# A bias added by one-partition matmuls into PSUM instead of by VectorE, in the spatial gate of a fused two-block kernel

## The chip, the cores and the metric

The kernel runs on one core of a Trainium2 chip. The metric is the device time of one execution in microseconds (us), as the median of several runs.

## The reference

The reference runs two network blocks on a sequence of 1024 tokens with 1024 channels. The first block has attention, a bidirectional mLSTM and a mixture of experts. The second block has an even layer and an odd layer. The change touches one part of the even layer, the spatial gate. With `u`, `v` and `g_b` as column groups of `rmsnorm(x) @ w_in`, of 1024 columns each:

```
vg = v.reshape(Bn, nc, CHUNK, B_GROUPS, B_GROUP_DIM)      # 8 chunks of 128 tokens, 4 groups of 256 channels
w = where(tril, ws, 0)                                     # (4, 128, 128)
mixed = einsum('gts,bnsgc->bntgc', w, vg) + bs.T[None, None, :, :, None]
y_b = u * mixed * silu(g_b)
x = x + concat([y_a, y_b]) @ w_out
```

The bias `bs[g, t]` depends on the group and on the token's place in its chunk, and is the same for all channels of the group.

## The kernel before, in words

`phase_even` is written with one hand-ordered instruction queue for each engine, tied by semaphores. Activations are channel-major: 128 channels in the partitions, 1024 tokens in the free dimension.

**The projection.** The input projection is cut into `PAIRS = 20` pairs of 128-channel tiles. Each pair `m` is computed as seven "products" of half-size blocks (a Strassen-like scheme, class `Quarters`). GpSimd (POOL) and ScalarE (ACT) split the weights into a high and a low part; TensorE (PE) runs 12 matmuls of 128x512 for each product (L2619 to L2621); ACT takes out the first product (`p1`) and VectorE (DVE) the others (`u2`, `u3`, `c21`, `c22_u4`, `c11`, `c12`, all L2635). Four PSUM banks take the products in turn, so a late eviction on DVE can hold up PE.

**The order of pairs.** Pairs 0 to 7 belong to the pooling part. Then there are four "triples" `j` (one for each spatial group), pairs `8+3j` (`v_cm`), `9+3j` (`g_cm`) and `10+3j` (`u_cm`). Small work is put between the products of these pairs:

- behind products 0 and 1 of the second pair, PE transposes `v` chunk by chunk (`turn_v`, L3017) into the PSUM tiles `aux` and `acc`, and DVE copies them to `v_rows_` (L3298);
- behind products 1 to 4 of the third pair, PE calls `mix_spatial(j, t, b)` (L3026), 16 calls in all. Each call runs four f32 matmuls of 128x128 with 128 moving columns, one for each of four chunks, into one bank;
- in the first pair of the next triple, DVE runs `gate_spatial` (L3304, `u * silu(g)`) and `mixed_out` for `t = 0, 1`: one add of the bias (L3312), which reads PSUM and writes `g_cm`, and one multiplication (L3315), into `gated`. For the last triple this stands behind all products, and `lo_of_y` (L3319) follows it, which makes the low parts that the out-projection (L3065) reads.

**The bias.** At the start of the phase one matmul with a ones row as weights (L2992) spreads the bias over all 128 partitions in `aux[:, 0]`. DVE copies it to `bias_rows` (L3335) between `u3(0)` and `c21(0)`, next to the copy of the transposed mixing weights (L3336).

**The out-projection.** It runs 16 units of 48 matmuls. The third unit (k = 2) is the first to need rows 8 to 15 of y, the last two of which come from the last triple.

Of the kernel before, what the change touches and what calls it, by code (L numbers as in the profile page):

```python
# [16 lines left out]
ALU = mybir.AluOpType  # L17
# [3 lines left out]
P = 128  # L21
LINE = 128
D = 1024
KT = D // P
# [9 lines left out]
CHUNK = 128  # L34
XCH = SEQ // CHUNK
# [14 lines left out]
CONST_AT, _n = {}, 0  # L50
# [106 lines left out]
class PhaseSemaphores:  # L157
# [25 lines left out]
    def sem(self, name):  # L183
        self.used.append(self.nc.alloc_semaphore(name, num=self.sets[0][len(self.used)]))
        return self.used[-1]

def build_program(nc, A, out):
    with ExitStack() as ctx:
        phases = PhaseSemaphores(nc)  # L190
        sem = phases.sem
# [10 lines left out]
        start = (nc.sbuf_base + LINE - 1) // LINE * LINE  # L202
# [20 lines left out]
        def cst(name):  # L223
            at, width = CONST_AT[name]
            return const[:, at:at + width]
# [9 lines left out]
        ident, ones = cst("ident"), cst("ones")  # L235
# [2446 lines left out]
        def phase_even(first_z):  # L2682
# [4 lines left out]
            G, POOL_PAIRS, TRIPLES = len(POOL_SIZES), 2 * len(POOL_SIZES), KT // 2  # L2687
# [39 lines left out]
            ws_t = mem("spat_ws_t", [P, G, CHUNK])  # L2727
# [3 lines left out]
            ws_low = ws_mem("spat_ws_low", [P, G, CHUNK])  # L2731

            v_cm = Arena(nc, a_at[0])("spat_v_cm", [P, 2, SEQ])
            v_rows_ = Arena(nc, a_at[1])("spat_v_rows", [P, 2, XCH, P])
            g_cm = Arena(nc, sums_at)("spat_g_cm", [P, 2, SEQ])
            u_cm = Arena(nc, pooled_at)("spat_u_cm", [P, 2, SEQ])
            gated = Arena(nc, y_at)("spat_gated", [P, 2, SEQ])
            bias = Arena(nc, start + 4 * CONST_AT["near_mask"][0])("spat_bias", [1, G, CHUNK])
            bias_rows = Arena(nc, start + 4 * CONST_AT["near_mask"][0])("spat_bias_rows", [P, G, CHUNK])
            assert G * CHUNK <= CONST_AT["near_mask"][1] + CONST_AT["chunk_mask"][1]  # L2740

            KO, EARLY = 2 * KT, 3
# [48 lines left out]
            masked = sem("spat_masked")  # L2792
            ws_turned = sem("spat_ws_turned")
            ws_ready = sem("spat_ws_ready")
            bias_out = sem("spat_bias_out")
            biased = sem("spat_biased")
            v_turned = sem("spat_v_turned")
            rows_out = sem("spat_rows_out")
            spat_silu = sem("spat_silu_done")
# [3 lines left out]
            y_done = sem("even_y_done")  # L2803
# [37 lines left out]
            def unit(k):  # L2841

                if k < 4:
                    return k % 2, KT * (k // 2)
                return k // 2, KT * (k % 2)

            with nc.psum_tensor("even_z", [P, 2, HALF], F32) as second_z, nc.psum_tensor("even_aux", [P, 2, HALF], F32) as aux, \
# [94 lines left out]
                def _(pe):  # L2942
# [45 lines left out]
                    spread_out(3)  # L2988
                    pe.wait_ge(masked, 1)
                    for g in range(G):  # L2990
                        pe.transpose(aux[:, 1, g * CHUNK:(g + 1) * CHUNK], ws_low[:, g, :], ident)
                    pe.matmul(aux[:, 0, :], ones[0:1, :], bias[:].rearrange("p g t -> p (g t)"), start=True, stop=True).then_inc(ws_turned, 1)  # L2992

                    def multiply(m, i, between=None):
                        if m == 0:
# [24 lines left out]
                    def mix_spatial(j, t, b):  # L3020
                        to = (aux, acc)[t]
                        pe.wait_ge(rows_out, 2 * j + t + 1)
                        if j == 0:
                            pe.wait_ge(ws_ready, 1)
                        for c in range(4):
                            ins = pe.matmul(to[:, b, c * CHUNK:(c + 1) * CHUNK], v_rows_[:, t, 4 * b + c, :], ws_t[:, j, :], start=(c == 0), stop=(c == 3))  # L3026
                        if b == 1:
                            ins.then_inc(spat_mixed, 1)

# [21 lines left out]
                    for k in range(2 * KT):  # L3051
                        n, first = unit(k)
# [6 lines left out]
                        for kt in range(KT):  # L3059
                            c = first + kt  # L3060
                            if k in (0, 2):
                                pe.wait_ge(y_lo_done, c + 1)
                            for w, rhs, begin, end in ((wo_hi, y_hi[c], c == 0, False), (wo_hi, y_lo[c], False, False), (wo_lo, y_hi[c], False, c == KO - 1)):
                                for b in range(2):
                                    ins = pe.matmul(z[n % 2][:, b, :], w[:, u, kt], rhs[:, b * HALF:(b + 1) * HALF], start=begin, stop=end)  # L3065
# [3 lines left out]
                def _(act):  # L3069
# [44 lines left out]
                    for m in range(PAIRS):  # L3114
                        g, j, kind = m // 2, (m - POOL_PAIRS) // 3, (m - POOL_PAIRS) % 3
                        if m == 0:
                            act.wait_ge(pads_clear, 1)
                        if m < POOL_PAIRS and m % 2 == 0 and g >= 2:
                            act.wait_ge(pooled_done, 2 * (g - 1))
                        if m < POOL_PAIRS and m % 2:  # L3120
                            act.wait_ge(y_done, 2 * g)
                        if m >= POOL_PAIRS:
                            if j == 0:
                                act.wait_ge((pooled_done, pooled_done, y_done)[kind], (2 * (G - 1), 2 * G, KT)[kind])
                            elif kind == 0:
                                act.wait_ge(v_turned, 2 * j)
                            else:
                                act.wait_ge(gated_done, j)
                            if j and kind == 1:

                                act.wait_ge(y_done, KT + 2 * j)
                        quarters.p1(act, m, banks, targets(m))
                        hi(m, 0)
                        if m < POOL_PAIRS + 1 and m % 2 == 0 and m:
                            act.wait_ge(quarters.evicted, 7 * (m - 1) + 7)
                            act.activation(silu[:], silu[:], ACT.Silu).then_inc(pool_silu, 1)
                        if m >= POOL_PAIRS and kind == 2:
                            act.wait_ge(quarters.evicted, 7 * (m - 1) + 7)
                            act.activation(g_cm[:], g_cm[:], ACT.Silu).then_inc(spat_silu, 1)
                        hi(m, 1)  # L3140
                        hi(m, 2)
                        if m < POOL_PAIRS and m % 2 and g:
                            store_y(2 * (g - 1), y)
                        if m >= POOL_PAIRS and kind == 1:
                            if j == 0:
                                store_y(KT - 2, y)
                            else:
                                store_y(KT + 2 * (j - 1), gated)
                        hi(m, 3)
                        hi(m, 4)  # L3150
                        hi(m, 5)
                        hi(m, 6)
# [32 lines left out]
                def _(dve):  # L3185
# [120 lines left out]
                    def mixed_out(j, t):  # L3306
                        dve.wait_ge(spat_mixed, 2 * j + t + 1)
                        dve.wait_ge(gated_done, j + 1)
                        if j == 0:
                            dve.wait_ge(bias_out, 1)  # L3310
                        mixed = g_cm[:, t, :]
                        dve.tensor_tensor(mixed.rearrange("p (c t) -> p c t", t=CHUNK), (aux, acc)[t][:].rearrange("p b (c t) -> p (b c) t", t=CHUNK),  # L3312
                                          bias_rows[:, j, :].unsqueeze(1).to_broadcast([P, XCH, CHUNK]), ALU.add).then_inc(biased, 1)
                        dve.wait_ge(biased, 2 * j + t + 1)
                        dve.tensor_tensor(gated[:, t, :], mixed, gated[:, t, :], ALU.mult).then_inc(y_done, 1)  # L3315

                    def lo_of_y(c):
                        dve.wait_ge(y_hi_done, c + 1)
# [2 lines left out]
                    for g in range(G):  # L3321
                        m = 2 * g
                        u2(m)
                        if g == 0:
                            token_lo(B21, b21)
                        u3(m)
                        if g == 0:
                            token_lo(B22, b22)

                            dve.wait_ge(t_lo_done, 7)  # L3330
                            step(dve.memset(sums[:, :, 0:PAD], 0.0))
                            step(dve.memset(a_pad[1][:, :, 0:PAD], 0.0))
                            dve.wait_ge(ws_turned, 1)
                            dve.wait_ge(x_stored, 16 * GROUPS)
                            dve.tensor_copy(bias_rows[:], aux[:, 0, :].rearrange("p (g t) -> p g t", g=G)).then_inc(bias_out, 1)  # L3335
                            dve.tensor_copy(ws_t[:], aux[:, 1, :].rearrange("p (g t) -> p g t", g=G)).then_inc(ws_ready, 1)  # L3336
                        c21(m)
                        c22_u4(m)
                        c11(m)
                        if g:  # L3340
                            gate_pool(g - 1)
                        c12(m)
                        m = 2 * g + 1
                        pool_part(g, 0)
                        u2(m)
                        pool_part(g, 1)
                        u3(m)
                        pool_part(g, 2)
                        c21(m)
                        pool_part(g, 3)  # L3350
                        c22_u4(m)
                        pool_part(g, 4)
                        c11(m)
                        pool_part(g, 5)
                        c12(m)
# [1087 lines left out]
```

## Time and profile before

| | |
|---|---|
| median of 3 runs | 3379.95 us (3379.56 to 3381.2) |
| profiled execution | 3379.95 us, span 3377.9 us |
| PE busy | 3125.4 us, 93% of the span |
| DVE busy | 1851.4 us, 55% |
| ACT, POOL busy | 38%, 48% |
| mean granted TensorE clock | 0.962 of full speed |
| even layer's first product to its last out-projection matmul | 1256.46 to about 1877 us of the span |

The span runs from the first to the last instruction of the profiled execution. Busy shares are averages over stages with different limits, so the stretch of the change has to be read by itself. PE matmuls are pipelined: a record of 0.39 us can start 0.23 us after the one before, so costs are read from distances between starts, not from durations. Records that follow one another are merged, with their count (x8). A f32 matmul shows as two records (two passes), and a f32r one or a transpose as one.

### The profile page before, as it was taken

The page shows a single profiled execution, that of the slowest core. Times are in us where ns is not written, and L with a number is a line of the kernel's source. Part 1 is how long each engine was busy: PE and PEld are TensorE (multiplying, and loading weights), DVE is VectorE, ACT ScalarE, POOL GpSimd, SP SyncE. Part 2 cuts the span into 40 slices and gives each one's busy share as a digit, 9 for nine tenths or more (in the row PEclk, how much of TensorE's full clock was granted, in tenths as well). Part 3 has the DMA queues.
Part 4 walks back from the last instruction along what each step waited for, and adds up shares of the span by engine and source line. Part 5 has one row for each costly group of instructions (what it writes and reads, how often), then busy time and mean ns, then how long its engine had stood idle before and what let it go on. Part 6 is the DMA issues. An engine that isn't in the chain of part 4 may idle for free. (4 is left out here: it accounts for less than half of the span.)

```text
span 3377.9 us, 43503 instructions
## 1 busy us (share of the span) xinstructions
PE 3125.4 (93%) x15972; PEld 2573.3 (76%) x15972; DVE 1851.4 (55%) x2678; ACT 1269.4 (38%) x2146; POOL 1611.9 (48%) x1056
## 2 busy tenths in 40 slices
PE   4979997969599969999999799999999999999999
PEld 3767786757388837778888588888888888888887
DVE  5566223662699856544361665555556556555712
ACT  5256122741477732222220343443344444222311
POOL 2331231123312217777743465565566556688732
PEclk8989998979799979999999899999999999999999
DMA  8230112035599961222251111111111111222331
GB/s 291 47 88 21 49 43 78 28 105 195 187 378 396 395 193 54 74 67 81 72 187 64 50 48 47 54 51 44 48 48 51 50 41 54 82 63 81 110 106 69
DMA packets 312571, 353.89 MB, mean 105 GB/s; under 512 B 28488, under 2 KB 280300, under 8 KB 306101
## 3 DMA queue, kind: packets, MB, share of 16 engines
q1 hardware_dynamic: 301182, 311.36, 27.5%
q0 software_dynamic: 4608, 16.78, 2.0%
q10 hardware_dynamic: 6582, 23.13, 1.7%
q8 instruction: 123, 2.02, 0.2%
q14 instruction: 76, 0.61, 0.1%
HBM read 293.28 MB, written 54.53 MB: 103 GB/s over the span
## 5 line engine op out<-in xcount | busy, mean ns | idle before, releaser
L2584 POOL TENSOR_TENSOR odd_quarter_lo<-odd_w_sums,odd_quarter_hi 128x512 fp32r<-128x512 f32 x224 | 300.3, 1342 | 278.2 <-ACT odd_quarter_hi L2579 276.7
L2619 PE MATMUL first_z<-odd_t_hi,odd_quarter_hi 128*128 128x512 f32 x784 | 327.5, 418 | 18.1 <-DVE odd_t_lo L4073 18.1
L2619 PE MATMUL odd_z<-odd_t_hi,odd_quarter_hi 128*128 128x512 f32 x784 | 325.5, 415 | 1.1 <-POOL odd_quarter_lo L2584 1.1
L2584 POOL TENSOR_TENSOR odd_quarter_lo<-odd_raw,odd_quarter_hi 128x512 fp32r<-128x512 f32 x168 | 232.0, 1381 | 167.4 <-ACT odd_quarter_hi L2579 163.0
L2621 PE MATMUL first_z<-odd_t_hi,odd_quarter_lo 128*128 128x512 f32 x784 | 308.3, 393 | 0.0
L2620 PE MATMUL first_z<-odd_t_lo,odd_quarter_hi 128*128 128x512 f32 x784 | 307.1, 392 | 0.0
L2621 PE MATMUL odd_z<-odd_t_hi,odd_quarter_lo 128*128 128x512 f32 x784 | 307.0, 392 | 0.0
L2620 PE MATMUL odd_z<-odd_t_lo,odd_quarter_hi 128*128 128x512 f32 x784 | 305.5, 390 | 0.0
L2579 ACT CAST odd_quarter_hi<-odd_w_sums 128x512 fp32r<-128x512 f32 x224 | 139.7, 624 | 365.6 <-PE odd_z L2621 178.8
L2635 DVE SCALAR_TENSOR_TENSOR dil_set<-first_z,dil_set 128x512 f32<-128x512 f32 x196 | 170.6, 884 | 143.3 <-PE first_z L2621 138.8
L2635 DVE SCALAR_TENSOR_TENSOR dil_set<-odd_z,dil_set 128x512 f32<-128x512 f32 x196 | 170.7, 884 | 138.4 <-PE odd_z L2621 133.5
L2579 ACT CAST odd_quarter_hi<-odd_raw 128x512 fp32r<-128x512 f32 x168 | 104.5, 622 | 293.9 <-PE first_z L2621 149.3
L275 POOL TENSOR_TENSOR w_hi<-w_raw,zero_col 128x1024 fp32r<-128x1024 f32 x25 | 47.4, 1895 | 303.1 <-PE mls_z L310 205.4
L2619 PEld LDWEIGHTS first_z<-odd_t_hi,odd_quarter_hi 128*128 128x128 f32 x784 | 148.5, 189 | 45.1 <-DVE odd_t_lo L4073 18.9
L2621 PEld LDWEIGHTS first_z<-odd_t_hi,odd_quarter_lo 128*128 128x128 f32 x784 | 148.2, 189 | 32.9
L2621 PEld LDWEIGHTS odd_z<-odd_t_hi,odd_quarter_lo 128*128 128x128 f32 x784 | 147.0, 187 | 32.5
L2620 PEld LDWEIGHTS first_z<-odd_t_lo,odd_quarter_hi 128*128 128x128 f32 x784 | 148.8, 190 | 26.9
L2619 PEld LDWEIGHTS odd_z<-odd_t_hi,odd_quarter_hi 128*128 128x128 f32 x784 | 147.6, 188 | 27.4 <-POOL odd_quarter_lo L2584 1.5
L2620 PEld LDWEIGHTS odd_z<-odd_t_lo,odd_quarter_hi 128*128 128x128 f32 x784 | 147.8, 189 | 26.5
L2584 POOL TENSOR_TENSOR even_quarter_lo<-even_w_sums,even_quarter_hi 128x512 fp32r<-128x512 f32 x80 | 110.5, 1385 | 72.0 <-ACT even_quarter_hi L2579 70.8
L2335 POOL DMA_INDIRECT ffn_rows<-expert_y,slot_token x16 | 32.6, 2040 | 219.6 <-ACT expert_y L2437 219.6
L4151 DVE COPY dil_p_t<-odd_aux 128x128 f32<-128x128 f32 (+1 forms) x192 | 67.6, 352 | 121.0 <-PE odd_aux L3736 100.2
(602 smaller groups left out, 8213.8 us busy)
## 6 DMA issues: line engine op xcount, KB each, us to landing
odd_raw<-in_odd_w_in SPq DMA_DIRECT2D x224, 256.0 KB, 3.1
raw_gate<-in_w_gate SPq DMA_DIRECT2D x16, 2048.0 KB, 15.0
raw_up<-in_w_up SPq DMA_DIRECT2D x16, 2048.0 KB, 14.8
raw_down<-in_w_down SPq DMA_DIRECT2D x16, 2048.0 KB, 15.2
even_raw<-in_even_w_in SPq DMA_DIRECT2D x80, 256.0 KB, 3.3
start_w_mod<-in_w_mod SPq DMA_DIRECT2D x11, 1024.0 KB, 10.8
w_raw<-in_w_in SPq DMA_DIRECT2D x16, 512.0 KB, 5.2
scan_w_mod<-in_w_mod SPq DMA_DIRECT2D x8, 1024.0 KB, 11.2
```

The source lines that it names most:

```text
L275: pool.tensor_tensor(w_hi[:, u], w_raw[:, u], zero_col[:, 0:1].to_broadcast([P, KT * P]).rearrange("p (k n) -> p k n", k=KT), ALU.add).the ...
L2335: pool.indirect_dma_start(ffn_rows, bass.IndirectOffsetOnAxis(ap=slot_token[:, e:e + 1], axis=0), y[:, e % 2, :], None, bounds_check=SEQ - ...
L2579: act.copy(self.w_hi[:, n % self.SLOTS], self.source(m, i)).then_inc(self.hi_done, 1)
L2584: pool.tensor_tensor(self.w_lo[:, n % self.SLOTS], self.source(m, i), self.w_hi[:, n % self.SLOTS].bitcast(F32), ALU.subtract).then_inc(se ...
L2619: pe.matmul(to, self.w_hi[:, slot, kt], t_hi[:, kt], start=(kt == 0), stop=False)
L2620: pe.matmul(to, self.w_hi[:, slot, kt], t_lo[:, kt], start=False, stop=False)
L2621: ins = pe.matmul(to, self.w_lo[:, slot, kt], t_hi[:, kt], start=False, stop=(kt == KT // 2 - 1))
L2635: dve.scalar_tensor_tensor(out=out, in0=product, scalar=scale, in1=more, op0=ALU.mult, op1=ALU.add).then_inc(self.evicted, 1)
L4151: dve.tensor_copy(p_t[:, u % 2, 0:w], turned[:, 0:w]).then_inc(free, 1)
```

## The change

The bias is no longer spread at the start of the phase and added by DVE. Each `mix_spatial` call first runs four matmuls that write the bias into the same PSUM places (weights: one row of 128 ones in one partition; moving data: the 128 bias values of group `j` in that partition), and then its four matmuls accumulate onto them. `mixed_out` keeps one instruction, a multiplication that reads PSUM. The matmul and the copy that spread the bias, the tile `bias_rows`, two semaphores and one wait of ACT are gone.

```diff
@@ PE, start of the phase
                     for g in range(G):
-                        pe.transpose(aux[:, 1, g * CHUNK:(g + 1) * CHUNK], ws_low[:, g, :], ident)
-                    pe.matmul(aux[:, 0, :], ones[0:1, :], bias[:].rearrange("p g t -> p (g t)"), start=True, stop=True).then_inc(ws_turned, 1)
+                        ins = pe.transpose(aux[:, 1, g * CHUNK:(g + 1) * CHUNK], ws_low[:, g, :], ident)
+                    ins.then_inc(ws_turned, 1)
@@ PE, mix_spatial
                         for c in range(4):
-                            ins = pe.matmul(to[:, b, c * CHUNK:(c + 1) * CHUNK], v_rows_[:, t, 4 * b + c, :], ws_t[:, j, :], start=(c == 0), stop=(c == 3))
+                            pe.matmul(to[:, b, c * CHUNK:(c + 1) * CHUNK], ones[0:1, :], bias[:, j, :], start=(c == 0), stop=False)
+                        for c in range(4):
+                            ins = pe.matmul(to[:, b, c * CHUNK:(c + 1) * CHUNK], v_rows_[:, t, 4 * b + c, :], ws_t[:, j, :], start=False, stop=(c == 3))
@@ ACT, main loop
-                            if j and kind == 1:
-
-                                act.wait_ge(y_done, KT + 2 * j)
@@ DVE, mixed_out
-                        if j == 0:
-                            dve.wait_ge(bias_out, 1)
-                        mixed = g_cm[:, t, :]
-                        dve.tensor_tensor(mixed.rearrange("p (c t) -> p c t", t=CHUNK), (aux, acc)[t][:].rearrange("p b (c t) -> p (b c) t", t=CHUNK),
-                                          bias_rows[:, j, :].unsqueeze(1).to_broadcast([P, XCH, CHUNK]), ALU.add).then_inc(biased, 1)
-                        dve.wait_ge(biased, 2 * j + t + 1)
-                        dve.tensor_tensor(gated[:, t, :], mixed, gated[:, t, :], ALU.mult).then_inc(y_done, 1)
+                        dve.tensor_tensor(gated[:, t, :], (aux, acc)[t][:].rearrange("p b n -> p (b n)"), gated[:, t, :], ALU.mult).then_inc(y_done, 1)
@@ DVE, start of the phase
                             dve.wait_ge(x_stored, 16 * GROUPS)
-                            dve.tensor_copy(bias_rows[:], aux[:, 0, :].rearrange("p (g t) -> p g t", g=G)).then_inc(bias_out, 1)
                             dve.tensor_copy(ws_t[:], aux[:, 1, :].rearrange("p (g t) -> p g t", g=G)).then_inc(ws_ready, 1)
```

## Rows read from the trace of the kernel before

**Rows 1.** The page: span, and PE's granted clock in 40 slices.

```profile
span 3377.9 us, 43503 instructions
...
PEclk8989998979799979999999899999999999999999
```

**Rows 2.** The triples: length, busy us (records) of PE, PEld, DVE, ACT, POOL; PEclk; DMA.

```profile
1470.00:1702.00 232.00, 232.00 (x1120) 194.79 (x1119) 93.42 (x106) 64.09 (x96) 166.92 (x118) 1.00 0.26 84
```

**Rows 3.** Waits of PE alone, 1300 to 1875: us in total, times, longest.

```profile
PE even_acc L3007 <- issue: 1.0, 1, 1.0
PE even_z L2619 <- POOL even_quarter_lo L2584: 0.4, 1, 0.4
```

**Rows 4.** Timeline around the first mix_spatial call: start us, us, engine, line.

```profile
1497.07 1.09 PEld L3026 LDWEIGHTS even_aux<-spat_ws_t,spat_v_rows 128*128 128x128 f32 x8
1497.30 1.06 PE L3026 MATMUL even_aux<-spat_ws_t,spat_v_rows 128*128 128x128 f32 x8
...
1498.11 0.48 PE L2619 MATMUL first_z<-even_t_hi,even_quarter_hi 128*128 128x512 f32 x1
...
1498.42 0.40 PE L2620 MATMUL first_z<-even_t_lo,even_quarter_hi 128*128 128x512 f32 x1
```

**Rows 5.** Timeline, DVE: evictions that wait for products of the third pair.

```profile
1508.44 1.29 DVE L2635 SCALAR_TENSOR_TENSOR spat_u_cm<-even_z,spat_u_cm 128x512 f32<-128x512 f32 x2 [2.95 <-PE even_z L2621]
...
1512.08 0.69 DVE L2635 SCALAR_TENSOR_TENSOR spat_u_cm<-even_z,spat_u_cm 128x512 f32<-128x512 f32 x1 [2.35 <-PE even_z L2621]
...
1514.80 0.69 DVE L2635 SCALAR_TENSOR_TENSOR spat_u_cm<-first_z,spat_u_cm 128x512 f32<-128x512 f32 x1 [2.03 <-PE first_z L2621]
```

**Rows 6.** Timeline, PE, start of the phase: matmuls on thin operands.

```profile
1228.72 3.61 PE L2956 MATMUL even_aux<-even_sq,const 128*1 128x256 f32 x16
...
1250.78 1.12 PE L2992 MATMUL even_aux<-spat_bias,const 1*128 1x512 f32 x2
1256.46 0.80 PE L2619 MATMUL first_z<-even_t_hi,even_quarter_hi 128*128 128x512 f32 x1 [4.56 <-DVE even_t_lo L3211]
```

**Rows 7.** Instructions by tile: count, ns min/median/max, first and last start.

```profile
L2992 PE MATMUL even_aux<-spat_bias,const x2: 587/640/692, 1250.8 to 1251.3; 1*128 1x512 f32 x2
...
L3315 DVE TENSOR_TENSOR spat_gated<-spat_g_cm,spat_gated x8: 1225/1724/1906, 1524.9 to 1715.1; 128x1024 f32<-128x1024 f32 x8
...
L3312 DVE TENSOR_TENSOR spat_g_cm<-even_aux,spat_bias_rows x4: 1217/1218/1225, 1523.6 to 1711.4; 128x1024 f32<-128x1024 f32 x4
```

**Rows 8.** Timeline, the first mixed_out, an eviction behind it, ACT's next p1.

```profile
1523.64 1.22 DVE L3312 TENSOR_TENSOR spat_g_cm<-even_aux,spat_bias_rows 128x1024 f32<-128x1024 f32 x1
...
1533.84 0.69 DVE L2635 SCALAR_TENSOR_TENSOR spat_v_cm<-even_z,spat_v_cm 128x512 f32<-128x512 f32 x1 [1.75 <-PE even_z L2621]
...
1536.64 0.60 ACT L2632 ACTIVATE spat_g_cm<-first_z 128x512 f32<-128x512 f32 x1 [2.18 <-PE first_z L2621]
```

**Rows 9.** Timeline, three engines, around the copy of the bias.

```profile
1284.53 0.69 DVE L3335 COPY spat_bias_rows<-even_aux 128x512 f32<-128x512 f32 x1
...
1286.90 1.28 POOL L2584 TENSOR_TENSOR even_quarter_lo<-even_raw,even_quarter_hi 128x512 fp32r<-128x512 f32 x1
...
1288.24 0.50 PE L2619 MATMUL even_z<-even_t_hi,even_quarter_hi 128*128 128x512 f32 x1 [0.75 <-POOL even_quarter_lo L2584]
```

**Rows 10.** Timeline behind the last product: third and fourth out-projection unit, last y_lo.

```profile
1711.40 1.23 DVE L3312 TENSOR_TENSOR spat_g_cm<-even_aux,spat_bias_rows 128x1024 f32<-128x1024 f32 x1
...
1725.67 6.25 DVE L3319 TENSOR_TENSOR even_y_lo<-spat_gated,even_y_hi 128x1024 fp32r<-128x1024 f32 x2
...
1724.30 0.61 PE L3065 MATMUL first_z<-even_y_hi,even_wo_hi 128*128 128x512 f32 x2
...
1735.22 0.62 PE L3065 MATMUL even_z<-even_y_hi,even_wo_hi 128*128 128x512 f32 x2
```

**Rows 11.** Stretches, PE alone: length, busy us (records), PEclk, DMA share, GB/s.

```profile
1250.00:1252.00 2.00, 1.90 (x8) 0.98 0.00 0
1256.00:1262.00 6.00, 5.49 (x12) 0.50 0.55 167
```

More of the change, by code:

```diff
@@ L2738, in phase_even @@
             bias = Arena(nc, start + 4 * CONST_AT["near_mask"][0])("spat_bias", [1, G, CHUNK])
-            bias_rows = Arena(nc, start + 4 * CONST_AT["near_mask"][0])("spat_bias_rows", [P, G, CHUNK])
-            assert G * CHUNK <= CONST_AT["near_mask"][1] + CONST_AT["chunk_mask"][1]
             KO, EARLY = 2 * KT, 3
@@ L2794, in phase_even @@
             ws_ready = sem("spat_ws_ready")
-            bias_out = sem("spat_bias_out")
-            biased = sem("spat_biased")
             v_turned = sem("spat_v_turned")
```

## The prediction

> **What bounds the kernel now.** I read the page first: its span, and the granted clock of TensorE by slices, which from the sixteenth slice on is at 9 (the full level of 2.4 GHz) in all slices but one [rows 1]. Then the stretch of the change in the even layer, to see which engine is full where the change acts. Between 1470 and 1702 us, the four triples, PE is busy for 232.00 of 232.00 us at a granted clock of 1.00, while DVE is busy for 93.42, ACT for 64.09 and POOL for 166.92 [rows 2]. Then the waits of PE by themselves from 1300 to 1875 us: two, 1.4 us together, neither behind a DVE instruction [rows 3]. So in the stretch of the change PE is the bound, and the other engines run behind it. Last I looked at single calls on the timeline, to price one pass of a small f32 matmul.
>
> The change gives PE work and takes work from DVE. All follows from that: what is added lies where nothing hides it, and what is removed lies under PE.
>
> **The cost on PE.** Four f32 matmuls are added to each of 16 `mix_spatial` calls: 64 matmuls. A call's four matmuls stand in the trace as eight records [rows 4], so 64 matmuls are 128 passes, each with a weight load of its own.
>
> What is a pass worth? I take it three ways.
> - By starts: the eight passes begin at 1497.30, and the second matmul of the next product at 1498.42 [rows 4]. That is 1.12 us, of which one ordinary product matmul is 0.227 (a product of 12 matmuls takes 1514.80 - 1512.08 = 2.72 us [rows 5]). It leaves 0.895 us for eight passes, 0.112 each.
> - By cadence: with a call between, a product's end comes 1512.08 - 1508.44 = 3.64 us after the last; without one, 2.72 [rows 5]. The call costs 0.92 us, 0.115 a pass. 
> - Low bound: the changeover lies within that cost. If all of the difference between the next product's first two starts (1498.11 and 1498.42 [rows 4], 0.31 us) and 0.227 is changeover, about 0.085 us, the eight passes are worth 0.81 us, 0.101 each.
>
> Those passes have 128 rows; the new ones have one. The nearest row is the matmul that is removed, which has the very same weights (one row of ones) and the same data in one piece. Its two passes of 512 columns take 1.12 us together [rows 6], with 0.587 to 0.692 for one record [rows 7]. So the distance between their starts is 0.43 to 0.53 us, and for 128 columns 0.107 to 0.133. Its granted clock was 0.98 [rows 11], so this is at the same level. A second thin shape, with one column of weights, takes 3.61 us for 16 passes of 256 columns [rows 6], with one record at 0.38 some 0.215 apart, or 0.107 for 128 columns. Neither thin shape is cheaper by columns than a full one; columns count, not rows. I take 0.112 us.
>
> 128 x 0.112 = 14.3 us. Bounds: 128 x 0.101 = 12.9, and 128 x 0.133 = 17.0 us.
>
> The Trainium skill gives the sustained distance for a stream of load and matmul pairs with 128 moving columns as about 81 ns (page "TensorE: Matmul & The Clock Gate", section "Back-to-back issue gap"); by that the sum would be an estimated 128 x 0.081 = 10.4 us. The figure is for one-pass data, and the trace of this kernel has 0.112 for a pass of f32; the row decides.
>
> **What is removed on PE.** The spreading matmul, 1.12 us at 1250.78 [rows 6], goes. PE then waits for `token_lo` on DVE until 1256.46 [rows 6], which the removal doesn't move: zero. If that wait were gone, it would be worth 1.1 us.
>
> **What is removed on DVE.** Eight adds of 1.22 us, 9.7 us; eight waits for them of 0.03 to 0.04, 0.3 us. The eight multiplications now take one operand from PSUM. I price them at the 1.22 us of the add, which also reads PSUM, instead of a median of 1.72 (two operands in SBUF) [rows 7]: some 4.0 us less. The copy of the bias is 0.6 us by starts [rows 9]. Together 14.6 us of DVE time, and on the path 0:
> - In the first three triples, the work of `mixed_out` starts at 1523.64, and DVE has caught up at 1533.84, where it waits 1.75 us for a product again [rows 8]. In between it was late, but PE did not wait for a bank [rows 3]. The cover is PE's own stream through four banks.
> - The last triple's adds lie behind all products, at 1711.40, and lead to the low parts of rows 14 and 15 of y, done at 1731.9. The third out-projection unit starts at 1724.30 and takes 10.92 us, or 1.365 for each row of y, so it needs the last row at 1724.30 + 7 x 1.365 = 1733.9 [rows 10]. That is 2.0 us of slack already. DVE waits there for PE's products, which come later by the added passes together with the unit, so the slack only grows. If it were gone, 2.9 us would be at stake.
> - The copy sits ahead of `c21(0)`. PE's next stop, at 1288.24, is released by POOL's split of 1286.90, not by an eviction [rows 9]. Zero; 0.6 us if it were an eviction.
>
> ACT loses a wait for `y_done`. The first one it stood ahead of begins at 1536.64, behind 2.18 us of waiting for PE's product [rows 8], so nothing is released. No DMA is added or moved; the loads of weights and of y go by PE's progress and shift with it. Behind the even layer everything hangs on the end of PE's last unit, and so the delay is carried to the end in full.
>
> **The sum.** The profiled execution took 3379.95 us, which is also the median of the runs shown; its span is 3377.9, with 2.05 us around it. 3379.95 + 14.3 - 0 = 3394.3 us. With the bounds: 3392.9 to 3397.0.
>
> **The rivals.**
> - *DVE gives it back.* If the evictions behind `mixed_out` did hold PE up through the banks, in each triple and at the end, the 14.6 us would come back: 3379.95 + 14.3 - 14.6 = 3379.7, no change. This decides only if PE has idle time of that size in the triples. It has none that the trace shows [rows 2, 3]. Matmul ends are modelled, so a hold of a few tenths could hide in a record, but the cadence of 2.72 us is that of undisturbed products [rows 5]. Chance 0.05, of which 0.02 on the faster side.
> - *Cheap passes.* If a pass over one partition ran at the rate of the product matmuls, 0.227 / 4 = 0.057 us for 128 columns [rows 5], the cost would be 7.3 us: 3387.2. For it: only one row of the array is fed. Against it: the removed matmul with the same operands [rows 6, 7]. Chance 0.05; it sits on the 0.2% line, so I halve it.
> - *Exposed weight loads.* If the loads did not run beside the matmuls of the other shape, each new pass would pay 0.187 us more (one load record of the call is 0.19, and eight spread over 1.09 us beside the matmuls [rows 4]): 128 x (0.112 + 0.187) = 38.3 us, 3418.2. In this kernel the loads do overlap where all rows are in use, since eight passes fit into less time than eight load durations. The Trainium skill says that weight loads overlap with matmuls in flight only when their row group differs (same page, "Part 3: Packing small matmuls", section "The mechanism"). A one-row matmul shares its row group with the full ones. The trace already contradicts the rule for full matmuls. Chance 0.03.
> - *The clock falls.* If the thin matmuls counted as rest and the granted clock went to its low level of 1.2 GHz behind each call, a product would take 5.49 instead of 2.72 us [rows 5, 11]: 16 x 2.8 + 14.3 = 59 us, 3439. At 1250 to 1252 us, with a thin matmul running, the clock was 0.98, and it was 0.50 only behind a gap of 4.6 us [rows 6, 11]. Chance 0.03.
>
> **How the numbers follow.** Forecast 0.84, rivals 0.16. A change within 0.2%, or 6.8 us, is about what a measurement of this kernel can't tell from none. Slower: 0.84 + 0.03 + 0.03 + 0.025 = 0.925. Same: 0.03 + 0.025 = 0.055. Faster: 0.02. The predicted time is the likeliest case, 3394.3. The range takes the bounds of the pass, 3392.9 and 3397.0, and about 2 us more on each side, a little over the spread of the runs shown (1.6 us): 3391 to 3399. It leaves out the rivals, 0.16.
>
> **What the profile after would show.** In the triples 128 new PE records of a one-row matmul, 8 ahead of each group of 8, and a distance between the product ends around a call of 3.64 + 0.90 = 4.54 us instead of 3.64. PE busy for all of the triples, its granted clock 1.00. The stretch from the first call to the end of the products is longer by 14.3 us; before and behind it, distances are as before. On DVE, L3312's adds are gone, the multiplications take 1.2 us, and its time without work is greater by about 14.3 + 14.6 = 28.9 us. Wrong would be: products that come closer together in the first pair of a triple than now (DVE did hold PE), passes 0.06 or 0.3 us apart, or a slice with a lower PEclk in the triples. A pass price other than 0.112 moves the sum by 1.28 us for each 0.01.

## The result, and the profile after

The changed kernel takes 3400.89 us (median of 4 runs, 3399.9 to 3401.98), the kernel before 3380.24 us (4 runs, 3379.56 to 3381.2) on the same chip. The ratio is 1.0061, with a 95% interval of 1.0046 to 1.0077. It is slower, as forecast, but by 20.7 us instead of 14.3, and 1.9 us above the range. The profiled execution took 3399.32 us.

The first two lines are the page's span and granted clock, and then come the stretch of the triples and the waits of PE in the even layer. They answer to [rows 1 to 3].

```profile
span 3397.2 us, 43746 instructions
...
PEclk8989998989799979999999899999999999999999
```

```profile
1470.00:1721.00 251.00, 251.00 (x1243) 207.93 (x1242) 82.10 (x99) 63.61 (x95) 162.12 (x119) 1.00 0.25 79
```

```profile
PE even_acc L3003 <- issue: 1.0, 1, 1.0
PE even_z L2619 <- POOL even_quarter_lo L2584: 0.4, 1, 0.4
```

PE is still busy for all of the triples, at a clock of 1.00, and has the same two waits as before. So there is no new wait and no lower clock: the added time is inside the stream of PE. From the first call to the first matmul of the out-projection it is 1721.14 - 1495.82 = 225.3 us; before, it was 205.2. That is 20.1 us more. The whole loss sits in the 16 calls. This stretch is a better measure than the span of one execution: the first call starts 1.5 us earlier here than before (1495.82 and 1497.30), and over all the traces of this document it starts anywhere from 1495.8 to 1502.4 us, whatever the calls cost.

How it is spread over them is seen on DVE, whose evictions wait for each product. These rows answer to [rows 5].

```profile
1500.84 0.69 DVE L2635 SCALAR_TENSOR_TENSOR spat_u_cm<-first_z,spat_u_cm 128x512 f32<-128x512 f32 x1 [4.22 <-PE first_z L2621]
...
1505.74 0.69 DVE L2635 SCALAR_TENSOR_TENSOR spat_u_cm<-first_z,spat_u_cm 128x512 f32<-128x512 f32 x1 [4.22 <-PE first_z L2621]
...
1515.56 0.69 DVE L2635 SCALAR_TENSOR_TENSOR spat_u_cm<-even_z,spat_u_cm 128x512 f32<-128x512 f32 x1 [3.62 <-PE even_z L2621]
...
1518.28 0.69 DVE L2635 SCALAR_TENSOR_TENSOR spat_u_cm<-first_z,spat_u_cm 128x512 f32<-128x512 f32 x1 [2.03 <-PE first_z L2621]
```

With a call between, products end 1505.74 - 1500.84 = 4.90 us apart (4.91 over the four calls of a triple), against 3.64 before and 4.54 forecast. Without a call it is 1518.28 - 1515.56 = 2.72 us, as before. A call costs 1.26 us more instead of 0.90, and 16 x 1.26 = 20.2 us.

Now one call from within: PE, and then PE's weight loads, around the first call. These answer to [rows 4].

```profile
1495.51 0.39 PE L2621 MATMUL even_z<-even_t_hi,even_quarter_lo 128*128 128x512 f32 x1
1495.82 1.15 PE L3022 MATMUL even_aux<-spat_bias,const 1*128 1x128 f32 x8
1496.91 1.16 PE L3024 MATMUL even_aux<-spat_ws_t,spat_v_rows 128*128 128x128 f32 x8
1497.82 0.48 PE L2619 MATMUL first_z<-even_t_hi,even_quarter_hi 128*128 128x512 f32 x1
...
1495.28 0.19 PEld L2621 LDWEIGHTS even_z<-even_t_hi,even_quarter_lo 128*128 128x128 f32 x1
1495.82 0.96 PEld L3022 LDWEIGHTS even_aux<-spat_bias,const 1*128 1x128 f32 x8 [0.35 <-issue]
1496.90 0.97 PEld L3024 LDWEIGHTS even_aux<-spat_ws_t,spat_v_rows 128*128 128x128 f32 x8
```

Three things are to be seen.

- Before, the first weight load of the call started 0.23 us ahead of its matmul, beside the matmuls of the product [rows 4]. Here the load of the bias starts at 1495.82 together with its matmul, with 0.35 us of idle time ahead, and the load of the first full matmul starts at 1496.90, 0.01 ahead. The loads don't run ahead where the weights go from 128 rows to one and back.
- The first bias matmul starts 0.31 us behind the last of the product, where 0.227 is the ordinary distance.
- The eight bias passes take 1496.91 - 1495.82 = 1.09 us instead of 0.895, and the eight full ones 1497.82 - 1496.91 = 0.91 instead of 0.81 [rows 4].

That is 0.08 + 0.195 + 0.10 = 0.38 us in all, about 0.19 for each of the two changes. The tile's rows say where a part of it sits (count, then ns at least, median and most):

```profile
L3022 PEld LDWEIGHTS even_aux<-spat_bias,const x64: 181/187/187, 1495.8 to 1704.6; 1*128 1x128 f32 x64
L3022 PE MATMUL even_aux<-spat_bias,const x64: 270/270/372, 1495.8 to 1704.7; 1*128 1x128 f32 x64
...
  issue: 5.6, 16
```

The first bias pass of a call takes 372 ns and the others 270; of the full passes behind them the first takes 377 and the others 275. The idle time of "issue" is 5.6 us in 16 pieces, one for each call.

On DVE the multiplication went as priced. These rows answer to [rows 8] and [rows 7]:

```profile
1527.13 1.21 DVE L3304 TENSOR_TENSOR spat_gated<-even_aux,spat_gated 128x1024 f32<-128x1024 f32 x1
1529.16 0.69 DVE L2635 SCALAR_TENSOR_TENSOR spat_v_cm<-first_z,spat_v_cm 128x512 f32<-128x512 f32 x1 [0.82 <-PE first_z L2621]
```

The multiplication takes 1.21 us (1.22 estimated), and DVE has caught up right behind it. At the tail, the last low parts of y and the start of the third out-projection unit, which answer to [rows 10]:

```profile
1741.42 2.35 DVE L3308 TENSOR_TENSOR even_y_lo<-spat_gated,even_y_hi 128x1024 fp32r<-128x1024 f32 x2
...
1742.90 0.62 PE L3063 MATMUL first_z<-even_y_hi,even_wo_hi 128*128 128x512 f32 x2
```

The low parts are done at 1743.8, and the last row of y is needed at 1742.90 + 7 x 1.365 = 1752.5. The slack grew from 2.0 to 8.7 us. A part of that was not priced: the two low parts take 2.35 us together, where they took 6.25 before [rows 10]. It is most of what DVE's busy time fell by beyond the forecast (1851.4 to 1832.7 us, 18.7 instead of 14.6). DVE is off the path, so it is worth nothing here, and no run asks for its cause.

### The profile page after: what moved, and what is told of

Its sections match the earlier page's. It is cut to its first block and busy times, and to the rows that moved or that the text cites. A ratio compares the mean times of both kernels' runs of the same rounds, so it can differ in the third digit from the quotient of the medians.

```text
span 3397.2 us, 43746 instructions
## 1 busy us (share of the span) xinstructions
PE 3144.3 (93%) x16098; PEld 2585.6 (76%) x16098; DVE 1832.7 (54%) x2669; ACT 1268.6 (37%) x2146; POOL 1598.9 (47%) x1056
```

## The experiments

All are edits of the changed kernel; the diffs show the lines that matter, and "..." stands for what is left out. Theory A, with its later forms, is that going over between weights of one row and of 128 costs time. The rivals were that accumulation onto a written bank costs, that a one-row pass is dear by itself, and that DVE's removed work was worth something. The measure of a call is the distance between product ends around it ("cadence": 3.64 before, 4.91 after).

**All 128 rows.** The same four bias matmuls with 128 rows of weights; rows 1 to 127 of the bias tile are zero.

```diff
+                    pool.memset(bias[:], 0.0).then_inc(bias_clear, 1)
...
-                            pe.matmul(to[:, b, c * CHUNK:(c + 1) * CHUNK], ones[0:1, :], bias[:, j, :], start=(c == 0), stop=False)
+                            pe.matmul(to[:, b, c * CHUNK:(c + 1) * CHUNK], ones[0:128, :], bias[0:128, j, :], start=(c == 0), stop=False)
```

> The changed kernel, but with the bias matmuls on all 128 rows: weights are the full tile of ones, and the moving tile holds the bias in row 0 and zeros in rows 1 to 127. Same count of passes and columns, same accumulation. Theory A (each change between one-row and 128-row weights costs about 0.19 us on PE, two for each of 16 calls, 6.1 us in all): the extra goes away, a call adds 0.90 us to the cadence, 16 x 0.90 = 14.3, so about 3394.7 us, 6 us below the changed kernel. Theory B (accumulating onto places just written costs the extra): no change from the changed kernel, 3400.9. Theory C (each one-row pass is itself slow, 1.26 / 8 = 0.158 us): also about 3394.7, so A and C are told apart by the next run.

3393.79 us (3391.38 to 3396.23, 5 runs) beside 3381.37 of before, 1.0037 (1.0023 to 1.0051). The cadence is 4.52. PE and the weight loads around its first call:

```profile
1497.45 0.39 PE L2621 MATMUL even_z<-even_t_hi,even_quarter_lo 128*128 128x512 f32 x1
1497.68 1.05 PE L3025 MATMUL even_aux<-spat_bias,const 128*128 128x128 f32 x8
1498.57 1.06 PE L3027 MATMUL even_aux<-spat_ws_t,spat_v_rows 128*128 128x128 f32 x8
1499.38 0.48 PE L2619 MATMUL first_z<-even_t_hi,even_quarter_hi 128*128 128x512 f32 x1
...
1497.46 1.08 PEld L3025 LDWEIGHTS even_aux<-spat_bias,const 128*128 128x128 f32 x8
```

The load runs 0.22 us ahead, the bias block takes 0.89 us and the full one 0.81. This is the forecast of the prediction (4.54), met with 128 times as many rows. Accumulation is ruled out as a cost, and so is the number of passes. What is left has to do with the one row.

**Two calls' bias together.** The call for bank 0 writes the bias of both banks, so that a pair of calls has two changes instead of four.

```diff
-                        for c in range(4):
-                            pe.matmul(to[:, b, c * CHUNK:(c + 1) * CHUNK], ones[0:1, :], bias[:, j, :], start=(c == 0), stop=False)
+                        if b == 0:
+                            for d in range(2):
+                                for c in range(4):
+                                    pe.matmul(to[:, d, c * CHUNK:(c + 1) * CHUNK], ones[0:1, :], bias[:, j, :], start=(c == 0), stop=False)
```

> The changed kernel, but the bias matmuls of both banks of a PSUM tile are issued together ahead of the first of the two calls: as many one-row passes as before, half as many blocks of them. Theory A (change of row count): 16 changes fewer, 16 x 0.19 = 3.0 us less, about 3397.8 us. Theory B (accumulation): the first call keeps it, the second has its places written earlier, so at most 8 x 0.19 = 1.5 us less. Theory C (slow one-row passes): no change, 3400.9.

3401.13 us (3399.63 to 3405.67, 5 runs), 1.006 (1.0047 to 1.0074): no gain, where theory A forecast 3397.8. Yet the cadences of the first triple are 5.81 and 3.64, or 9.45 for a pair against 9.81, which is the 0.36 of two changes saved. Eight pairs should have given 2.9 us. Where they went is seen in the stretches of PE in the second triple (length, busy us and records, clock, DMA share, GB/s):

```profile
1576.00:1578.00 2.00, 2.00 (x17) 1.00 0.00 0
1579.50:1582.00 2.50, 2.50 (x9) 0.50 0.80 225
1582.00:1584.00 2.00, 2.00 (x12) 0.99 0.37 112
```

Behind the 16 one-row passes the granted clock falls to 0.50, the level of 1.2 GHz, though PE never stopped, and it does so again in the third triple; behind the other six of the eight pairs it stays at 1.00. The stretch from the first call to the out-projection takes 225.6 us, where 225.3 - 2.9 = 222.4 was due, so the two falls cost 3.2 us. The saving is real and is given back by the clock.

**No bias at all.** The bias matmuls are left out, and with them the bias from the computation.

```diff
-                            pe.matmul(to[:, b, c * CHUNK:(c + 1) * CHUNK], ones[0:1, :], bias[:, j, :], start=(c == 0), stop=False)
```

> The changed kernel with the bias left out of the computation altogether: no bias matmuls, and the one multiplication on DVE as in the changed kernel. It shows what the removal on DVE is worth alone. Theory (DVE is off the path): the time of the kernel before, 3380.2 us, within 1. Rival (DVE gives time back): up to 14.6 us below it, 3365.6.

3382.27 us (3379.47 to 3385.76, 11 runs) beside 3381.37, 1.0004 (0.9994 to 1.0013), and the cadence is 3.65. In the trace the stretch from the first call to the out-projection is 205.24 us, that of the kernel before to the hundredth. The removed work of DVE, the spreading matmul and the wait of ACT are together worth nothing.

**One wide matmul.** The four bias matmuls as one of 512 columns, which reads the 128 values four times: two passes instead of eight, with the same columns.

```diff
-                        for c in range(4):
-                            pe.matmul(to[:, b, c * CHUNK:(c + 1) * CHUNK], ones[0:1, :], bias[:, j, :], start=(c == 0), stop=False)
+                        pe.matmul(to[:, b, :].rearrange("p (c t) -> p c t", t=CHUNK), ones[0:1, :], bias[:, j, :].unsqueeze(1).to_broadcast([1, 4, CHUNK]), start=True, stop=False)
```

> The changed kernel with the four bias matmuls of a call as one matmul over 512 columns, which repeats the 128 bias values four times through a stride of zero: 2 one-row passes instead of 8, the same number of columns. Theory A: two changes of row count stay, columns stay: 0.86 us of columns and 0.38 of changes, about 3400, at most 1 us below the changed kernel. Theory C (a fixed extra of 0.05 us for each one-row pass): 6 passes fewer in each call, 16 x 6 x 0.05 = 4.8 us less, about 3396.

3400.39 us (3399.64 to 3405.74, 5 runs), 1.0062 (1.0048 to 1.0075); the cadence is 4.89. The count of passes doesn't matter, and a single block still pays both changes. Its tile row is that of the matmul removed by the change [rows 7], to the digit:

```profile
L3021 PE MATMUL even_aux<-spat_bias,const x16: 587/640/692, 1498.8 to 1707.0; 1*128 1x512 f32 x16
```

**96 and 97 rows.** As with 128 rows, but with `ones[0:96]` and `bias[0:96]`, or 97. Any count other than 128 is a change of row count; if that alone were dear, both would be slow.

```diff
+                            pe.matmul(to[:, b, c * CHUNK:(c + 1) * CHUNK], ones[0:96, :], bias[0:96, j, :], start=(c == 0), stop=False)
```

> The bias matmuls on rows 0 to 95 of 128 (ones; the bias in row 0, zeros below). Theory A1 (a change between any two row counts costs 0.19 us): the cadence around a call stays near the 4.91 us of the changed kernel, whole time near 3400. Theory A2 (what counts is whether the same blocks of 32 rows are in use): three blocks of four, so also a change, 4.91 and 3400. Theory A3 (only a one-row or one-block load is slow to start): 4.52 and 3394.

> The bias matmuls on rows 0 to 96, one row more than e5, which touches the fourth block of 32 rows. Theory A1 (any change of row count): 4.91 us around a call and about 3400. Theory A2 (blocks of 32 rows): all four blocks are in use as in the full matmuls, so 4.52 us around a call as in e1, and about 3394.

3393.76 us (3393.44 to 3399.05, 5 runs) and 3395.45 us (3393.71 to 3399.53, 5 runs), beside 3381.3: 1.0038 (1.0025 to 1.0051) and 1.004 (1.0027 to 1.0053). Both cadences are 4.54, with no pass at 372 ns. A change of the row count alone costs nothing (4.52 with 128 rows).

**In turn.** One bias matmul, then one full matmul, and so on: eight changes in a call instead of two.

```diff
                         for c in range(4):
                             pe.matmul(to[:, b, c * CHUNK:(c + 1) * CHUNK], ones[0:1, :], bias[:, j, :], start=(c == 0), stop=False)
-                        for c in range(4):
                             ins = pe.matmul(to[:, b, c * CHUNK:(c + 1) * CHUNK], v_rows_[:, t, 4 * b + c, :], ws_t[:, j, :], start=False, stop=(c == 3))
```

> The changed kernel's 64 one-row matmuls, each directly ahead of its full matmul instead of four and then four: the same passes, but eight changes of row count in a call instead of two. Theory A: 0.90 + 8 x 0.19 = 2.42 us for a call, 16 calls 38.7 us, about 3419; the cadence around a call is 3.64 + 2.42 = 6.06 us. Theory B (accumulation onto places just written): only one matmul lies between, so a little more than 3401, without a count of its own. Theory C (slow one-row passes): no change, 3401.

3432.43 us (3427.22 to 3434.59, 5 runs), 1.0144 (1.0131 to 1.0158). The cadences of the first triple are 7.66, 7.66, 6.06 and 6.10; 6.06 is the forecast (3.65 + 0.90 + 8 x 0.19 = 6.07). The two long ones come from the clock. PE in and behind the first call, and the clock of the stretches:

```profile
1500.28 0.48 PE L3022 MATMUL even_aux<-spat_bias,const 1*128 1x128 f32 x2
1500.69 0.49 PE L3023 MATMUL even_aux<-spat_ws_t,spat_v_rows 128*128 128x128 f32 x2
1501.11 0.48 PE L3022 MATMUL even_aux<-spat_bias,const 1*128 1x128 f32 x2
...
1502.87 0.63 PE L2619 MATMUL first_z<-even_t_hi,even_quarter_hi 128*128 128x512 f32 x1
1503.30 0.63 PE L2620 MATMUL first_z<-even_t_lo,even_quarter_hi 128*128 128x512 f32 x1
...
1500.00:1513.00 13.00, 13.00 (x47) 0.74 0.07 21
1513.00:1530.00 17.00, 17.00 (x79) 1.00 0.16 48
```

Each block of two passes takes 0.41 us, where 2 x 0.112 = 0.22 would be free of changes: 0.19 each, at full clock. Then ordinary product matmuls stand 0.43 us apart instead of 0.227. The clock fell to 0.50 eight times in the triples, behind two calls of each. The stretch from the first call to the out-projection takes 256.8 us instead of the 205.2 + 38.7 = 243.9 forecast, so the falls cost 12.9 us.

**The same with 128 rows.** The order of the last one, the weights of the first.

```diff
+                            pe.matmul(to[:, b, c * CHUNK:(c + 1) * CHUNK], ones[0:128, :], bias[0:128, j, :], start=(c == 0), stop=False)
```

> e7 with the bias matmuls on all 128 rows: one bias matmul and one full matmul in turn, the same count of passes and of alternations, but no change of mode. Theory A4: the cadence around a call is 4.52 us as in e1, the granted clock stays at 1.00 in the triples, about 3394 us. Rival (the alternation of tiles or places costs, whatever the rows): near e7's 3432 us.

3394.61 us (3394.12 to 3398.8, 4 runs) beside 3380.77, 1.0043 (1.0026 to 1.006); the cadence is 4.52 and the clock in the triples 1.00. Alternation as such costs nothing and doesn't lower the clock. Both effects need the thin operands (a matmul's weights and moving data have the same rows, so the runs can't part the two).

**32, 64 and 65 rows.** Where does it begin? The edit is that of 96 rows with another number.

> The bias matmuls on rows 0 to 31. e5 and e6 showed that 96 and 97 rows cost as little as 128, so not any change of row count counts. Theory A4 (the array runs in a mode of 32, 64 or 128 rows, and a change of the mode stops the weight load from running ahead): 32 rows are a mode of their own, so the cadence around a call is 4.91 us as with one row, and the time near 3400. Rival A5 (only a single row is special): 4.52 to 4.54 us and about 3394.

> The bias matmuls on rows 0 to 63. Theory A4 (modes of 32, 64 and 128 rows): 4.91 us around a call, near 3400. Rival A5: 4.54 us, about 3394. A third possibility, that only loads of up to 32 rows are special: 4.91 for e9 and 4.54 here.

> The bias matmuls on rows 0 to 64, one more than e10. Theory A4: 65 rows need the full mode of 128, so no change of mode: 4.54 us around a call and about 3394, as with 96 and 97. If the cost went down step by step with the rows, it would lie close to that of 64.

32 rows: 3402.05 us (3399.99 to 3402.61, 4 runs), 1.0062 (1.0045 to 1.0078), cadence 4.91. 64 rows: 3400.62 us (3399.13 to 3401.19, 4 runs), 1.0056 (1.004 to 1.0073), 4.95. 65 rows: 3394.3 us (3393.55 to 3396.5, 5 runs), 1.0039 (1.0024 to 1.0053), 4.54. The loads of the call with 64 rows:

```profile
1496.22 0.19 PEld L2621 LDWEIGHTS even_z<-even_t_hi,even_quarter_lo 128*128 128x128 f32 x1
1496.76 0.96 PEld L3025 LDWEIGHTS even_aux<-spat_bias,const 64*128 64x128 f32 x8 [0.35 <-issue]
```

And with 65 rows, loads and matmuls:

```profile
1498.97 0.19 PEld L2621 LDWEIGHTS even_z<-even_t_hi,even_quarter_lo 128*128 128x128 f32 x1
1499.20 1.09 PEld L3025 LDWEIGHTS even_aux<-spat_bias,const 65*128 65x128 f32 x8
...
1499.42 1.05 PE L3025 MATMUL even_aux<-spat_bias,const 65*128 65x128 f32 x8
```

One row more, and the load runs ahead again; 6.3 us are gone (16 x 0.41 = 6.6 by the cadences). Nothing in the kernel differs but this count. The edge is between 64 and 65 rows, and 1, 32 and 64 rows are alike to 0.04 us.

The stretch of PE from the first call to the first matmul of the out-projection, in the trace of each run, says the same for all 16 calls together:

| bias matmuls | stretch, us |
|---|---|
| none (kernel before; without bias) | 205.24; 205.24 |
| 128 rows; 128 rows in turn | 219.22; 219.21 |
| 97, 96 and 65 rows | 219.54 each |
| 64 rows | 225.95 |
| 32 rows; one row (the change) | 225.32; 225.32 |

The Trainium skill has this rule: under "Mode switching requires drain" (page "TensorEngine Tiling (Array Packing)", section "Key Properties") it says that a change of the tiling mode drains TensorE; the row modes, 128, 64 and 32, are in its section "Available Configurations". The traces fit it, with about 0.19 us for a change each way, for f32 matmuls of 64 rows or fewer although nothing is packed. They don't show the drain itself, nor more than 0.04 us between 32 and 64 rows, nor a change between these two; that the edge is one of modes is read from the page. The runs show only that it lies between 64 and 65.

**One wide matmul of f32r.** Can the idea be had without the cost? The bias is cut into a high and a low part, in rows 0 and 32 of a zeroed tile of 128 rows. One f32r matmul (one pass) of 512 columns with 128 rows of ones adds both.

```diff
-                        for c in range(4):
-                            pe.matmul(to[:, b, c * CHUNK:(c + 1) * CHUNK], ones[0:1, :], bias[:, j, :], start=(c == 0), stop=False)
+                        pe.wait_ge(bias_ready, 2)
+                        pe.matmul(to[:, b, :].rearrange("p (c t) -> p c t", t=CHUNK), ones_r[:], bias_r[:, j, :].unsqueeze(1).to_broadcast([P, 4, CHUNK]), start=True, stop=False)
```

> A cheaper form of the change that keeps its purpose: bias as a f32r high part in row 0 and a f32r low part in row 32 of a zero-filled 128-row tile, weights a f32r tile of ones, one matmul of 512 columns for each call (the 128 values repeated four times), one pass. By the passes of the products, 0.227 us for 512 columns and no change of row count: 16 x 0.227 = 3.6 us over the kernel before, about 3384 to 3385, and a cadence of 3.87 us around a call. Rival: the change from f32r to f32 matmuls costs more in this order, up to 0.09 us a call, 3386.

3383.33 us (3378.47 to 3388.77, 11 runs) beside 3381.3, 1.0003 (0.9994 to 1.0012). PE in its first call:

```profile
1502.40 0.40 PE L3036 MATMUL even_aux<-spat_bias_r,spat_ones_r 128*128 128x512 f32 x1
1502.64 1.06 PE L3038 MATMUL even_aux<-spat_ws_t,spat_v_rows 128*128 128x128 f32 x8
```

The cadence is 3.87, 0.23 above the kernel before; 16 calls cost 3.6 us. It can't be told from the kernel before by its time, and by its stretch in the trace it is 3.6 us longer. No version that was run beats the kernel before.

## Why the prediction was right in its direction and wrong in its size

- **What bounds the kernel:** right. PE had no wait in the triples before or after, and each added microsecond of PE came out at the end: 20.1 us in the stretch, 20.7 in the medians.
- **What a pass is worth:** right. At 128, 97, 96 and 65 rows the calls cost 0.88 to 0.90 us more, or about 0.11 a pass, and the time rises by 12.4 to 14.2 us (14.3 forecast). For one row, the run with two calls' bias together tells it free of changes: its call has eight one-row passes more than one of the changed kernel and takes 5.81 - 4.91 = 0.90 us more, 0.112 each. Columns count and rows don't, for the pass itself.
- **The changeover: the step that failed.** "This holds the cost of changing over from f32r to f32 and back, which the added matmuls don't pay again, because they stand beside f32 matmuls." That is true of the data type, and the run with 128 rows shows it. But the added matmuls also went from 128 rows to one and back, and this change was costed at nothing, without a reason. It measures 0.19 us each way, or 16 x 0.38 = 6.1 us. With it the sum is 3379.95 + 14.3 + 6.1 = 3400.4, against 3400.89 measured.
- **The row that showed it** was read past. The removed thin matmul stands with 587/640/692 ns [rows 7]. The two durations, 0.105 us apart, were taken as an uncertainty of the price, when the longer one was the first pass behind a change. The passes start 0.53 us apart (1250.78 and 1251.31), of which 0.10 is the change and 0.43 the columns, 0.107 for 128 of them. The trace before also had the other sign, a weight load that starts with its matmul and not ahead of it:

```profile
1250.77 0.29 PEld L2992 LDWEIGHTS even_aux<-spat_bias,const 1*128 1x128 f32 x2 [0.17 <-issue]
```

The run with one wide matmul has the same 587 and 692 in 16 calls, and the changed kernel has 270 and 372, the same 0.10 us.
- **DVE gives it back** (0.05): dead. Without the bias the kernel takes the time of before, so the removed work was worth 0, as forecast (a stretch of 205.24 us in both traces).
- **Cheap passes** (0.05): dead, by the passes above.
- **Exposed weight loads** (0.03): the nearest to the truth, and wrong in how often. It charged 0.187 us to each of 128 passes; about that much is paid at the 32 changes. Loads of one-row weights do run beside one-row matmuls: eight passes with loads of 0.187 us stand in 1.09 us. The Trainium skill's rule on row groups (page "TensorE: Matmul & The Clock Gate", section "The mechanism") doesn't fit as it stands: loads of 128 rows run beside matmuls of 128 rows, and loads of one row beside matmuls of one row. What the traces tell apart is whether the row count crosses the edge between 64 and 65.
- **The clock falls** (0.03): not in the changed kernel. But it was no idle thought: with the one-row matmuls drawn together or alternated the clock fell to 0.50 beside a full PE, two and eight times. The argument from the stretch with a clock of 0.98 [rows 11] held for a single thin matmul alone.
- **The range:** its bounds came from three readings of the same full-row call and from one thin matmul. The full-row call has no change between thin and full rows. The thin matmul has one, and the upper bound of 0.133 a pass holds it; but spread over the passes as a price for columns, it stood for 2.7 us (17.0 - 14.3) instead of 6.1.

Open: which part of the 0.19 us is the load that can't run ahead (0.19 us by itself), and whether the drain that the page names has a part in it. No run parts them. Nor do the runs say why the clock falls behind some calls and not behind others of the same form.

## What to carry to other kernels

Where a f32 matmul of 64 or fewer rows is put into a stream of full ones, count its passes by columns and add about 0.4 us for each time in and out; a tile filled up with zero rows to 65 or more avoids that at no cost in passes. Look at the first record behind a change of shape by itself: the spread of a few records (587 against 692 ns) can be a cost with a place, and not noise. And where PE is full, work on DVE that nobody waits for is free, so moving it to PE can only cost; the cheapest form found, one f32r matmul in all rows, still costs its columns.

## What the runs showed of the hardware that was not expected

- Between 64 and 65 rows of weights the cadence drops from 4.95 to 4.54 us. With 1, 32 or 64 rows behind 128, the weight load no longer runs ahead of the matmuls, and the first pass takes 0.37 instead of 0.27 us; in and out cost about 0.19 us each.
- Above the edge, changes of row count are free: 96, 97 and 65 rows beside 128 have a cadence of 4.54 us, and 128 rows 4.52.
- The granted clock fell to 0.50 with PE busy without a break, behind 16 one-row passes in a row (two of eight times, 3.2 us in all) and behind one-row and full matmuls in turn (eight of 16 times, 12.9 us in all). The same order with 128 rows kept 1.00.
